# Joining the stages of a two-layer hybrid diffusion block: fewer program blocks, norms that begin chunk by chunk, masks made in the projection

## The reference

```
hx = modulate(rms_norm(x, norm1_w[i]), mx[0], mx[1])        # the context likewise
q, k, v, ... = split_proj(hx, w_in[i])                      # one input projection
o_ret = bidirectional retention (6 heads of 64, chunks of 128 tokens):
    diff = pos[:, None] - pos[None, :]
    decay_mask = where(diff >= 0, exp(log_gamma * max(diff, 0)), 0)
    scores = einsum(q, k) * decay_mask ;  cross = (q * q_decay) @ state
o_mla, o_gqa = softmax attention, 4 and 6 heads
x = x + mx[2] * (concat(o_ret, o_mla, o_gqa) @ w_out[i])
x = x + mx[5] * conv_ffn(modulate(rms_norm(x, norm2_w[i]), mx[3], mx[4]))
# after both layers:
return rms_norm(x, final_norm_w)

rms_norm(x, w) = x * rsqrt(mean(x * x) + EPS) * w
modulate(h, shift, scale) = h * (1 + scale) + shift
conv_ffn(h) = (silu(gate) * val) @ w_down, with (gate, val) = depthwise_conv3(h @ w_up), D_FF = 2816
```

## Time and profile before

| | |
|---|---|
| median of 3 runs | 3526.21 us (3524.91 to 3526.29) |
| the profiled execution | 3527.06 us, of which the span from first to last instruction 3525.3 us |
| PE matmul busy | 3403.9 us, 97% of the span |
| PE weight loads | 2880.9 us, 82% |
| DVE busy | 2402.3 us, 68% |
| ACT busy | 1266.6 us, 36% |
| POOL busy | 776.0 us, 22% |
| mean granted clock of PE | 0.988 of full speed |

### The profile page before, as it was taken

How to read it: one execution, slowest core, us unless ns; L and a number is a source line. 1 busy time by engine, 2 the same in 40 slices (tenths; PEclk the granted TensorE clock), 3 DMA queues, 4 the chain that set the end, 5 groups by cost and what they waited for, 6 DMA issues and landing times. The chain is left out here.

```text
span 3525.3 us, 49033 instructions
## 1 busy us (share of the span) xinstructions
PE 3403.9 (97%) x18304; PEld 2880.9 (82%) x18304; DVE 2402.3 (68%) x3517; ACT 1266.6 (36%) x2140; POOL 776.0 (22%) x368
## 2 busy tenths in 40 slices
PE   7999899999989999999999999899999999999997
PEld 4888788888878888888888688789998788888885
DVE  6575567887189999988756533478993656656656
ACT  4332356666231111211123432356773322222223
POOL 1221210001412222222223211210013232222223
PEclk9999999999999999999999999999999999999998
DMA  5455462122122222222111424462212111111111
GB/s 229 152 186 199 126 193 68 52 68 68 30 79 72 71 71 71 71 71 71 36 36 30 160 91 157 135 187 62 53 52 78 43 48 42 54 48 42 54 48 48
DMA packets 95948, 304.22 MB, mean 86 GB/s; under 512 B 11584, under 2 KB 38336, under 8 KB 93632
## 3 DMA queue, kind: packets, MB, share of 16 engines
q1 hardware_dynamic: 95808, 302.33, 26.5%
HBM read 239.11 MB, written 63.18 MB: 86 GB/s over the span
## 5 line engine op out<-in xcount | busy, mean ns | idle before, releaser
L181 PE MATMUL up_acc<-h_hi,whi 128*128 128x512 f32 (+1 forms) x1735 | 642.7, 370 | 13.3 <-DVE h_lo L466 11.3
L182 PE MATMUL up_acc<-h_lo,whi 128*128 128x512 f32 (+1 forms) x1735 | 640.0, 369 | 0.0
L183 PE MATMUL up_acc<-h_hi,wlo 128*128 128x512 f32 (+1 forms) x1735 | 639.8, 369 | 0.0
L2144 DVE SCALAR_TENSOR_TENSOR xT<-down_acc,mod,xT 128x512 f32<-128x512 f32 (+1 forms) x800 | 515.9, 695 | 176.5 <-PE down_acc L183 174.1
L130 POOL TENSOR_TENSOR wlo<-raw,whi 128x1024 fp32r<-128x1024 f32 x133 | 341.1, 2565 | 1145.9 <-ACT whi L119 1145.9
L181 PEld LDWEIGHTS up_acc<-h_hi,whi 128*128 128x128 f32 x1735 | 328.1, 189 | 72.1 <-issue 10.3
L183 PEld LDWEIGHTS up_acc<-h_hi,wlo 128*128 128x128 f32 x1735 | 327.8, 189 | 55.0
L182 PEld LDWEIGHTS up_acc<-h_lo,whi 128*128 128x128 f32 x1735 | 328.1, 189 | 53.5
L2032 ACT ACTIVATE up<-up_acc 128x512 f32<-128x512 f32 (+1 forms) x210 | 115.8, 554 | 598.5 <-PE up_acc L183 598.2
L181 PE MATMUL down_acc<-hid_hi,first_whi 128*128 128x512 f32 (+1 forms) x825 | 311.9, 378 | 7.1 <-DVE xT L2144 4.0
L183 PE MATMUL down_acc<-hid_hi,first_wlo 128*128 128x512 f32 (+1 forms) x825 | 315.4, 382 | 0.0
(11 more groups left out here) (297 smaller groups left out, 6323.0 us busy)
## 6 DMA issues: line engine op xcount, KB each, us to landing
raw<-in_w_rest SPq DMA_DIRECT2D x112, 512.0 KB, 3.6
norm_buf<-in_w_ada SPq DMA_DIRECT2D x52, 768.0 KB, 4.5
first_raw<-in_w_rest SPq DMA_DIRECT2D x57, 512.0 KB, 3.7
proj_scratch<-stage SPq DMA_DIRECT2D x18, 640.0 KB, 4.1
raw<-in_w_first SPq DMA_DIRECT2D x21, 512.0 KB, 6.6
ada_raw<-in_w_ada SPq DMA_DIRECT2D x6, 1536.0 KB, 13.9
xT<-proj_scratch SPq DMA_DIRECT2D x4, 1920.0 KB, 8.9
xT<-in_xT SPq DMA_DIRECT2D x8, 640.0 KB, 24.9
```

The costliest lines, as they stand in the source:

```text
L181: nc.tensor.matmul(out, hi, xhi, start=start, stop=False)
L182: nc.tensor.matmul(out, hi, xlo, start=False, stop=False)
L183: return nc.tensor.matmul(out, lo, xhi, start=False, stop=stop)
L2144: nc.vector.scalar_tensor_tensor(xs, db[g % DB][:, :w], mod_of(layer, 5, m, c), xs, ALU.mult, ALU.add).then_inc(added, 1)
```

## The change

**Blocks.** `first_modulations` and the input projection of layer 0 become one block. In each layer retention, attention, output projection and MLP become one block, with the input projection of layer 1 behind the MLP of layer 0, and the final norm behind that of layer 1. The only joints of blocks left are those between an input projection and the retention after it, and `clear_semaphores` now stands there.

**Handing over.** A stage returns `Handed`, with the semaphores and functions by which the next one does the last squares, additions, totals and roots of its norm. The last group's work is thus queued among the next stage's first pieces, by dictionaries `between` from a piece's number to a function. The norm of a chunk waits for its own root alone (`self.rooted`). The buffers `hi` and `lo` are now shared by the stages (`mix_hi` for the first four pieces, `late_hi` for the other four). `totals` of the output projection now stand ahead of the fourth piece of the next chunk's group, that of the last chunk ahead of the fourth piece (layer 0) or the second piece (layer 1) of the MLP's opening pair. In the MLP `log` goes ahead of the square of piece 6 and `exp` behind all squares of the next chunk; in layer 0 the third chunk's root goes behind the second `hi` of the projection.

**Masks.** The twelve Exp and three POOL operations go from retention into the projection, at its tiles 15 and 16, with three small loads (retention's eight become six), and take the tables of cosines and sines as room. `decq` is made in the last three rounds.

The diff, cut to its core:

```diff
             for i, (c, t0, w) in enumerate(self.chunks):
                 for k in range(KB):
+                    if i * KB + k in between:
+                        between[i * KB + k]()
                     act.wait_ge(self.t_ready, i * KB + k + 1)
-                    nc.scalar.activation(self.hi[:, k, t0:t0 + w], self.t[:, k % 2, :w], ACT.Identity,
+                    nc.scalar.activation(self.hi[k][:, t0:t0 + w], self.turned(c, k), ACT.Identity,
                                          bias=mod_of(self.layer, self.shift_j, k, c)).then_inc(self.hi_done, 1)
...
             for n, (c, t0, w, k) in enumerate(work):
                 which = 1 if c == 0 else 0
+                if n in between:
+                    between[n]()
+                if k == 0:
+                    dve.wait_ge(self.rooted, n // KB + 1)
...
-                nc.vector.scalar_tensor_tensor(self.t[:, k % 2, :w], xT[:, k, t0:t0 + w],
+                nc.vector.scalar_tensor_tensor(self.turned(c, k), xT[:, k, t0:t0 + w],
                                                scale[:, k, which:which + 1], self.r[:, t0:t0 + w],
                                                ALU.mult, ALU.mult).then_inc(self.t_ready, 1)
...
+                sp.wait_ge(handed.squares, handed.summed)
                 if layer:
                     sp.dma_start(x_scratch[:, :, :], xT[:, :, :]).then_inc(x_kept, 16)
+                    sp.wait_ge(handed.total_done, len(chunks))
                 for dst, src in ((cos, a["cos64"]), (sin, a["sin64"]), (cos8, a["cos32"]), (sin8, a["sin32"]),
...
+                    if u == MASKS:
+                        sp.wait_ge(roped, rope_at["q2"] + 1)
+                        for dst, src in ((dist, a["ret_dist"]), (sides, a["ret_keep"]), (lg, a["ret_lg"][layer])):
+                            sp.dma_start(dst[:, :, :], src).then_inc(table_in, 16)
...
+                pool.wait_ge(mask_part, 2 * RH)
+                for d in range(2):
+                    nc.gpsimd.tensor_tensor(decay[d], decay[d], sides[:, d, :].unsqueeze(1).to_broadcast([P, RH, P]), ALU.mult).then_inc(mask_made, 1)
+                pool.wait_ge(mask_made, 2)
+                pool.wait_ge(roped, len(ROPES))
+                nc.gpsimd.tensor_tensor(small["mask"], decay[0], decay[1], ALU.add).then_inc(mask_made, 1)
...
-                nc.scalar.preload_act_table_set(LN_EXP)
-                norm.act(act, third_split)
+                def second_root():
+                    handed.root(act, 1)
+                def third_root():
+                    handed.root(act, 2)
+                norm.act(act, {2: third_root, 12: third_split} if layer else {1: second_root, 3: third_root, 12: third_split})
...
+                    if u in (MASKS, MASKS + 1):
+                        d = u - MASKS
+                        act.wait_ge(table_in, 48)
+                        for h in range(RH):
+                            nc.scalar.activation(decay[d][:, h, :], dist[:, d, :], ACT.Exp, scale=lg[:, h, d:d + 1]).then_inc(mask_part, 1)
...
+                if layer:
+                    dve.wait_ge(handed.made, 48 // 3)
...
-                pool.wait_ge(masks_made, 2 * RH)
-                for d, m in ((0, mask), (1, mtmp)):
-                    nc.gpsimd.tensor_tensor(m[:, :, :], m[:, :, :], small["keep"][:, d, :].unsqueeze(1).to_broadcast([P, RH, P]),
-                                            ALU.mult).then_inc(mask_made, 1)
-                pool.wait_ge(mask_made, 2)
-                nc.gpsimd.tensor_tensor(mask[:, :, :], mask[:, :, :], mtmp[:, :, :], ALU.add).then_inc(mask_made, 1)
...
-                tables = [(m, d, h) for d, m in ((0, mask), (1, mtmp)) for h in range(RH)]
-                tables += [(decq, d, t) for d in range(2) for t in range(3)]
...
-                    for dst, d, j in tables[2 * c:2 * c + 2]:
-                        if dst is decq:
-                            nc.scalar.activation(decq[:, d, j, :], small["qpos"][:, d, :], ACT.Exp, scale=small["lgp"][:, j, d:d + 1]).then_inc(decq_made, 1)
-                        else:
-                            nc.scalar.activation(dst[:, j, :], small["dist"][:, d, :], ACT.Exp, scale=small["lg"][:, j, d:d + 1]).then_inc(masks_made, 1)
+                    for d, t in tables[2 * (c - BLK + 3):2 * (c - BLK + 4)] if c >= BLK - 3 else []:
+                        nc.scalar.activation(decq[:, d, t, :], small["qpos"][:, d, :], ACT.Exp, scale=small["lgp"][:, t, d:d + 1]).then_inc(decq_made, 1)
...
-            banks = [banks[i] for i in (0, 1, 3, 4, 2, 5)]
+            order = (1, 4, 0, 3, 2, 5) if last else (0, 1, 3, 4, 2, 5)
...
-                for i in range(nch):
-                    square(KB - 1, i)
-                    if i:
-                        root(i - 1)
-                root(nch - 1)
+                        square(act, m, i)
+                square(act, KB - 1, 0)
+                root(act, 0)
+            def total(pe, i):
+                _, c0, w = chunks[i]
...
+                            if m == KB - 1 and i and kb == 3:
+                                total(pe, i - 1)
                             wk = slice(kb * P, (kb + 1) * P)
                             mm = three_pass(banks[g % 6][:, :w], whi[:, wk], wlo[:, wk],
...
-                        if m == KB - 1 and i:
-                            total(i - 1)
-                total(nch - 1)
...
+                            if i == 0 and kb == (1 if last else 3):
+                                handed.total(pe, nch - 1)
+                            if kb == 0:
+                                pe.wait_ge(handed.squares, max(handed.free[c], handed.free[3 + c]))
...
+                    act.wait_ge(handed.groups, handed.group_count)
                     ring.split_hi(act, 0, 0, base + AHEAD)
+                def square_last():
+                    handed.square(act, nch - 1)
+                def root_last():
+                    handed.root(act, nch - 1)
...
-                norm.act(act, third_split)
+                if last:
+                    norm.act(act, {2: square_last, 4: root_last, 9: third_split})
+                else:
+                    norm.act(act, {4: square_second, 7: root_second, 10: square_last, 12: root_last, 17: third_split})
...
-                        if i and m == KB - 1:
-                            root(i - 1)
+                        if i and m == KB - 2:
+                            log(act, i - 1)
                         square(i, m)
-                root(nch - 1)
+                    if i:
+                        exp(act, i - 1)
+                if last:
+                    root(act, nch - 1)
...
-                norm.dve(dve)
+                def add_second():
+                    handed.add(dve, 1)
+                def add_last():
+                    handed.add(dve, nch - 1)
+                norm.dve(dve, {2: add_last} if last else {4: add_second, 10: add_last})
...
+                for i, (c, t0, w) in enumerate(chunks):
+                    dve.wait_ge(handed.rooted, i + 1)
                     for k in first:
...
             if layer == 0:
+                opening = ExitStack()
+                block = opening.enter_context(nc.Block())
                 with Segment().open(a["w_first"], NTILE) as seg:
-                    first_modulations(seg)
-                    clear_semaphores()
-                    input_projection(0, last, seg, 0)
...
+                    opening.close()
                 seg.forget()
+                clear_semaphores()
...
+                late = [seg.sb(x, [P, KB - EARLY, TOK], f32r) for x in ("late_hi", "late_lo")]
+                hi, lo = ([x[:, k, :] for k in range(EARLY)] + [y[:, k, :] for k in range(KB - EARLY)]
+                          for x, y in zip((early.hi, early.lo), late))
+                handed = output_projection(layer, last, seg, hi, lo, unit, block, attended)
+                handed = mlp(layer, last, seg, KB, hi, lo, block, handed)
+                if last:
+                    final_norm(seg, block, handed)
+                else:
+                    input_projection(1, True, seg, mlp_end, hi, lo, block, handed)
                 joint.close()
-                mlp(layer, last, seg, KB)
+            if not last:
+                seg.forget()
                 clear_semaphores()
-                if last:
-                    final_norm(seg)
-                else:
-                    input_projection(1, True, seg, mlp_end)
-            seg.forget()
```

231 lines of the change are left out of this document (133 added, 98 removed).

## The result

The changed kernel takes **3506.77 us** in the median of four runs (3502.5 to 3507.82), before 3526.25; the ratio is 0.9946 with a 95% interval of 0.9934 to 0.9958, so it is 19.5 us faster. One execution of the kernel of experiment 6 took 7639.82 us, for a reason that nothing here shows; it is left out of the ratios. The forecast was 3494, with 3486 to 3502 as its range. The direction was right, but 13 of the 32.5 us did not come. The profiled execution took 3506.0 us, its span is 3503.9 us, 21.4 less than before.

A forecast was written before the change was run, and what follows sets the result against it. TensorE, busy 3403.9 of 3525.3 us, was taken as the bound, losing time to waits and low clock at joints between stages. Seven terms summed to 32.5 us, giving a median of 3494 us, range 3486 to 3502.

The forecast's parts named there:

- term 1: Joint from output projection to MLP, layer 0: norm starts with its own chunk's root, PE goes straight on; gain 9.6 us.
- term 2: Joint from output projection to MLP, layer 1: norm starts 6.4 us sooner, DVE sets the pace; gain 5.1 us.
- term 4: Opening to projection, layer 0: norm starts with chunk 0's root, less 1.5 us for the other roots; gain 3.0 us.
- term 6: Clearing semaphores moves to the two joints ahead of retention, where it lies open: a loss of 1.2 us.
- term 7: MLP to final norm: DVE starts with the first chunk's root and stays busy to its end; gain 5.6 us.
- Rival A: Queued roots and additions hold the norms back until the last total, so they gain only the switch: 3513 us; chance 0.05.
- Rival B: Moving the masks brings nothing, as POOL's query products stop DVE where the masks did: 3499.5 us; chance 0.08.
- rival D: More than the sum: DVE's and ACT's stalls at the joints hide behind each other, up to 8 us more, 3486; chance 0.09.
- Rival C: PE's clock falls to 1.2 GHz through the pairs that open stages: 90 us lost, 3584 us; chance 0.02.
- term 3: MLP of layer 0 to projection of layer 1: norm 7.5 us sooner, less a new 2.6 us stall; gain 4.9 us.
- Term 5: Masks moved out of retention: 3.0 us of PE's waits saved per layer, minus 0.5 in layer 0; gain 5.5 us.
- all else is order inside slack: Everything in the change outside the seven priced gains and losses was taken to cost nothing; no size or bound given.

The follow-up runs named there:

- experiment 6: The kernel before with nothing but 384 bytes put ahead of the buffers at the upper end of the memory: 3514.97 us, ratio 0.9972.
- experiment 7: The changed kernel with the output projection's last additions, squares, roots and total held ahead of the MLP's first piece, no barrier: 3521.46 us, ratio 0.9991.

## Why the prediction was right or wrong

**Right.** What bounds a joint (the norm's start and the stall at `wlo`) and how much of it goes. Terms 1, 2, 4, 6 and 7 came within 0.4 us of their values: term 1's stretch was worked out at 44.1 us and measured at 44.26, with the clock at 1.00; the held kernel shows that it is the start by chunks. Rival A is what the held kernel does, and the changed one does not: held at two of its joints it is 16 us slower, by the ratios. Rival B falls by the trace of retention and by the masks put back, rival D by the seven terms, which give 32.4 to 34.4 us where 32.5 were forecast.

**Right in the sum, not in the parts.** The half clock behind a joint was named as one of its costs, and experiment 7 shows that in layer 0 it cost nothing. Rival C did come, in small: 3 us at clock 0.50 in each of two pairs, 1.5 us together where its whole was 90. In term 3 DVE's last `lo` comes 4.86 us sooner after the last product's pass than before, just the 4.9 of the forecast, but PE's third tile only 3.7: 0.9 us of the difference is that clock. With the root four pieces later, and the clock at 1.00, the term is 6.8. In term 4 DVE's last `lo` is 3.5 us sooner and PE's third tile 2.8, so that the 3.0 was met is partly luck. Term 5 was 5.5 and is 8.0 between the two profiled executions, 6.0 at like clock. That nearness is luck too. In layer 0 the masks gave 4.5 us, not 3.0: the sum took the two waits in the earlier trace rows and left out that the rounds around them waited as well, 1.67 us ahead of the last `pa`, which became 0.76. In layer 1 they gave 1.5, since the loss by POOL's query products that was put in layer 0 came there, as the 3.09 us of `po`. By the rule of the Trainium skill ("SBUF — State Buffer", "🔬 SBUF: two separate sides"), with the three operations holding DVE for their whole length and PE with it, the term would have been 11.5; the trace has 6.0 to 8.0.

**The step that failed** is not in the seven terms. It is the sentence that all else is order inside slack. The change hands the output projection's `hi` and `lo` to the MLP and to the last projection, so half of the data of the up products lie in `mix_hi` and `mix_lo`, 128 bytes modulo 256 from their weights, where all had lain at 0; in the last projection half of the passes are so placed, where a third had been. The prediction read the diff for its order and its waits and not for its places, and gave this no term and no bound. It costs some 7 ns on each such pass of 0.23 us: 4.3 + 7.2 + 1.1 = 12.6 us in the stretches, nearer 14 at like clock, against the 13 us that are missing. The rows for it were there: the earlier trace rows begins with a pass from `mix_hi` in a group in which 12 such passes take 2.79 us (961.40 to 964.19), and in the same group those from `o_hi` take 2.75 us, and the groups by form had 394 against 390 ns. Had it been taken from them, 0.0033 us for each of half of 4224 up passes of 512 columns is 7 us, the sum 25.5, and the forecast 3501, inside the stated range and 6 us from the measured time; the price would still have been too low by half.

The range was too narrow for the same reason: it held errors of the terms that were named, and nothing for one that was not.

## What to carry to other kernels

When a change lets a stage use other buffers, compare the price of one instruction by form before and after, in a stage that the change "does not touch": on an engine that is busy 97% of the time, 1% there outweighs a joint. And before a term is called wrong by a microsecond or two, compare the granted clock of its stretch in both traces. For products, put data and weights at addresses within a partition that are equal modulo 256 bytes, as far as this kernel's forms go (float32 in three passes, 256 and 512 columns); here that alone was worth 10 us to the old kernel and, with the hidden columns and one root's place, 39 to the new one. And a norm that starts when its own chunk is ready is worth the wait that it ends; the barrier beside it was worth little.
